# Up projections by seven block products: the first layer too, and when gates, turns and down projections start

## The chip, the cores and the metric

The kernel runs on one core of a Trainium2 chip. The metric is the time of one execution in microseconds (us); shown beside it are the profiled execution and its span, from the first instruction to the last. The engines have short names in the views: PE is TensorE (PEld its weight loads), DVE VectorE, ACT ScalarE, POOL GpSimd, SP the engine that issues the weight loads; PS is the accumulator memory of 8 banks. All numbers are float32. A float32 matmul of the program is two records in the trace ("x16" is eight matmuls).

## The reference, cut to what matters

512 latent tokens of width 1024 pass four layers, and 256 context tokens go with them in layers 0 and 2. In each layer a mixer's output is projected ("out"), weighed by a gate and added; the tokens are normalised, modulated and pass a feed-forward part, whose result is again weighed by a gate and added. What the change touches is the feed-forward part and the gates:

```python
m = silu(c) @ w_mod[i] + b_mod[i]          # shifts, scales and two gates
h = layer_norm(ALPHA * h + g_m * (y @ w_out), ...)
f = square(relu(modulate(h, sh_f, sc_f) @ w1)) @ w2     # layers 0, 1: 1024 -> 4096 -> 1024
h = layer_norm(ALPHA * h + g_f * f, ...)
# layers 2, 3: rms_norm; up 1024 -> 2 * 2816, three-tap convolution along the tokens,
# silu(one half) * other half, down 2816 -> 1024; residual without ALPHA
```

Layer 0 does this for 768 tokens (6 tiles of 128), layer 1 for 512 (4 tiles), layer 2 for 768, layer 3 for 512. Layers 2 and 3 are the second block.

## The kernel before, in words

All weights come through RING, two slots filled in turn by SP; the load for a slot waits until the tile two places earlier is used. Every engine runs a list of its own in a fixed order, and they meet by semaphores: a *flow* is a set of PS buffers with a semaphore "full" (posted by PE) and one "free" (posted by DVE or ACT, first when that engine *offers* the flow).

**Out projection** (`both_halves`, L955 to L982; matmuls recorded at L971): output columns in two halves; in the second half, tile by tile, eight products k of 512 columns. After product k = 7 of tile t PE turns the normalised tile t-1 (`turn_tokens`, eight transposes, L863), which ACT writes to UT with shift and scale (`turned_tokens`, L2481, eight operations). DVE evaluates each tile (`residual`, L1788 and after): product by gate, addition, and for layers 0 and 1 the statistics, the root from ACT (L2488) and two passes of the norm; for layers 2 and 3 ACT squares the tile and takes the root (`rms`, L2557), then DVE scales it (L1860). ACT's order for layers 2 and 3 (`boundary`) is: rms of tile t, then turn of tile t-1. In layers 2 and 3 `conv_columns` (L984) stands behind product k = 3 of the last tile but one (layer 2) or the last (layer 3): PE waits until the tile turned last is in UT, transposes the convolution's vectors (L991), and waits until DVE has copied them (L1775).

**Up projection, layers 1 to 3** (`paired_up`, products at L1016): 256 output columns are a pair. Weights and tokens are cut in 2 by 2 blocks (K in two halves of 4 x 128, columns in two of 128, tokens in two halves), and seven products P1 to P7 stand for eight. PE gives P1 and P2 of pairs 0 and 1 first, with the turn of the last tile between; ACT copies P1 (L2498), and P2 waits for that. DVE makes four sums of tokens for each tile of the second half of the tokens (L2314 to L2317) and four sums of weights for each pair (L2303 to L2306, of pair 0 before the last tile's token sums), and PE's P6 waits for them. DVE then adds up the quarters with seven additions a pair (L2361 to L2377), counted by `quarters_taken`. In layer 1 ACT makes relu and square (L2901, L2902); in layers 2 and 3 DVE makes the convolution (`convolved`, L2338 to L2349).

**Up projection, layer 0** (`up`): eight weight tiles of 512 columns, four chunks each; a chunk is eight matmuls of 512 latent tokens (L926) and eight of 256 context tokens (L928), 32 chunks in all; ACT makes relu and square of 768 tokens (L2887, L2889). The first two chunks go in `early_tile` (L885), latents first.

**Down projection** (`both_halves` again, in four parts of the contraction for each half): PE waits at L1675 for `hidden_ready`, which ACT posts behind the last square (layers 0, 1) and DVE behind the last convolution (layers 2, 3).

**Gates of layer 0**: behind the attention PE transposes them (`gate_rows`, L853), ACT copies them (L2471), POOL stores them to DRAM (L3029) and reads them back on all partitions (L2954, four DMAs); DVE waits for that (L2398) before it offers the flow of the out projection. The attention runs over 40 units in 43 steps, and the rows the gates are made of are complete after step 24.

## Time and profile before

| what | us |
|---|---|
| median of three runs | 4323.12 |
| lowest, highest | 4320.63, 4330.89 |
| the profiled execution, its time | 4322.84 |
| its span | 4321.0 |
| PE busy | 4073.6 (94%) |
| DVE busy | 1690.2 (39%) |
| ACT busy | 813.0 (19%) |

The profile has one core. The page gives busy times and the chain of work that ended last; the chain in order of time gives the long stretches; the timeline shows single instructions, with the idle time of their engine before them in brackets and what ended it; the windows give the granted clock of TensorE in a stretch, 1.00 for 2.4 GHz and 0.50 for 1.2 GHz.

### The profile page before, as it was taken

Reading aid. Unit: us, or ns where it says so; the run is one execution under the profiler, and the core shown is the slowest. Engines: PE = TensorE matmul, PEld = TensorE weight load, DVE = VectorE, ACT = ScalarE, POOL = GpSimd, SP = SyncE. Lnnn points to the kernel's source line nnn. Section 1 sums busy time; section 2 is a strip of 40 time slices with the busy share of each in tenths; the row PEclk is TensorE's granted clock in tenths of the full one; section 3 lists DMA queues with packets and bytes.
Section 4 is the critical chain, followed back from the end, with each engine's and each line's share of the span. In section 5 each row is a group of like instructions: output and inputs, shape, how many; then the busy total and the mean of one; then the engine's idle time right before and its main releaser. Section 6 shows DMA issues by size and latency. Waiting matters only on the chain.

```text
span 4321.0 us, 44906 instructions
## 1 busy us (share of the span) xinstructions
PE 4073.6 (94%) x18144; PEld 2431.1 (56%) x18144; DVE 1690.2 (39%) x2856; ACT 813.0 (19%) x1549; POOL 239.9 (6%) x228
## 2 busy tenths in 40 slices
PE   7998999999999999999999997799998999989999
PEld 6676455544455555458646545545554444758854
DVE  0253400001256555544202028637775015437841
ACT  1265211100122222111102123321100021521000
POOL 1000000000013431300000000000000000000000
PEclk8999999999999999999999997899999999999999
DMA  4255111111112221322223112301111121002222
GB/s 177 102 184 175 49 59 39 58 39 59 33 69 88 81 86 69 118 68 88 88 78 108 38 42 103 133 21 59 59 59 49 54 71 65 1 21 88 87 80 73
DMA packets 192901, 325.68 MB, mean 75 GB/s; under 512 B 4146, under 2 KB 74104, under 8 KB 192576
## 3 DMA queue, kind: packets, MB, share of 16 engines
q1 hardware_dynamic: 186816, 302.00, 20.2%
q0 software_dynamic: 5888, 20.91, 1.5%
q8 instruction: 141, 2.31, 0.2%
q14 instruction: 56, 0.46, 0.0%
HBM read 320.74 MB, written 2.16 MB: 75 GB/s over the span
## 4 chain that ended last, share of the span: by engine, by line
PE 87%; DVE 7%; ACT 3%; issue 1%; DMA 1%; POOL 0%; DVEq 0%; ACTq 0%; SPq 0%
PE PS L971 26%; PE PS L1016 18%; PE PS L926 7%; PE PS L928 3%; PE PS L948 3%; PE PS L885 3%; PE PS L1471 3%; PE PS L1485 2%; PE PS L801 2%; PE PS L1472 1%; PE PS L1632 1%; PE PS L1642 1%; PE PS L1166 1%; PE PS L1135 1%; PE PS L1361 1%
## 5 line engine op out<-in xcount | busy, mean ns | idle before, releaser
L971 PE MATMUL PS<-RING,BIG 128*128 128x512 f32 x2352 | 1022.1, 596 | 22.4 <-DVEq L1721 16.0
L971 PEld LDWEIGHTS PS<-RING,BIG 128*128 128x128 f32 x2352 | 447.6, 191 | 579.8 <-issue 558.7
L1788 DVE TENSOR_TENSOR RES_TMP<-PS,GATE 128x512 f32<-128x512 f32 x80 | 55.3, 692 | 1404.6 <-PE PS L971 1332.5
L1016 PE MATMUL PS<-UT,RING 128*128 128x256 f32 (+1 forms) x1920 | 530.4, 424 | 31.5 <-ACT BIG L2498 15.0
L1016 PEld LDWEIGHTS PS<-UT,RING 128*128 128x128 f32 x1920 | 364.4, 192 | 170.3 <-DVE BIG L2367 22.7
L1016 PE MATMUL PS<-BIG,RING 128*128 128x256 f32 (+1 forms) x1440 | 396.8, 419 | 1.5 <-DVEq L1721 1.1
L926 PE MATMUL PS<-UT,RING 128*128 128x512 f32 x704 | 356.4, 593 | 1.0 <-ACT BIG L2674 1.0
L1016 PEld LDWEIGHTS PS<-BIG,RING 128*128 128x128 f32 x1440 | 273.2, 190 | 96.9 <-DVEq L1721 2.8
L928 PEld LDWEIGHTS PS<-UT,RING 128*128 128x128 f32 x656 | 124.6, 190 | 156.9 <-issue 156.9
L928 PE MATMUL PS<-UT,RING 128*128 128x256 f32 x656 | 195.1, 379 | 0.0
L971 PE MATMUL PS<-RING,UT 128*128 128x512 f32 x320 | 141.5, 601 | 15.7 <-DVEq L1701 14.0
L926 PEld LDWEIGHTS PS<-UT,RING 128*128 128x128 f32 x704 | 133.4, 190 | 30.0 <-issue 12.0
L948 PE MATMUL PS<-RING,UT 128*128 128x512 f32 x320 | 140.1, 600 | 2.5 <-ACT BIG L2766 0.9
L1471 PE MATMUL PS<-UT,RING 128*128 128x512 f32 x256 | 131.1, 594 | 3.3 <-DVE BIG L2126 1.9
L2481 ACT ACTIVATE UT<-PS,COL 128x128 f32<-128x128 f32 x328 | 118.8, 468 | 52.4 <-PE PS L863 49.2
L885 PE MATMUL PS<-UT,RING 128*128 128x256 f32 (+2 forms) x576 | 125.9, 380 | 1.4 <-ACTq L2438 1.4
L801 PE MATMUL PS<-RING,CVW 128*32 128x128 f32 x3072 | 103.5, 291 | 22.5 <-DMA RING<-w_mod_dram 15.7
L1485 PE MATMUL PS<-UT,RING 128*128 128x512 f32 x256 | 120.1, 594 | 0.0
L885 PEld LDWEIGHTS PS<-UT,RING 128*128 128x128 f32 x576 | 99.0, 190 | 26.3 <-issue 16.6
L2191 DVE SCALAR_TENSOR_TENSOR BIG<-PS,BIG 128x510 f32<-128x510 f32 (+3 forms) x176 | 110.5, 628 | 6.2
L971 PEld LDWEIGHTS PS<-RING,UT 128*128 128x128 f32 x320 | 61.0, 193 | 90.0 <-issue 89.4
L1323 PE MATMUL PS<-UT 64*128 64x128 f32 x672 | 73.1, 364 | 38.6 <-DVE GB L2073 24.9
(388 smaller groups left out, 4456.0 us busy)
## 6 DMA issues: line engine op xcount, KB each, us to landing
RING<-w_mod_dram SPq DMA_DIRECT2D x48, 2048.0 KB, 7.9
RING<-ff_w_dram SPq DMA_DIRECT2D x24, 2048.0 KB, 8.0
RING<-w_ffn_up_dram SPq DMA_DIRECT2D x44, 1024.0 KB, 5.0
RING<-ssm_w_in_dram SPq DMA_DIRECT2D x8, 2048.0 KB, 7.7
RING<-ff_w_dram SPq DMA_DIRECT2D x16, 1024.0 KB, 5.3
RING<-w_ffn_down_dram SPq DMA_DIRECT2D x8, 1536.0 KB, 6.6
RING<-w_ffn_down_dram SPq DMA_DIRECT2D x8, 1280.0 KB, 5.8
RING<-ssm_w_out_dram SPq DMA_DIRECT2D x4, 2048.0 KB, 7.8
```

What stands on the lines that cost most here:

```text
L801: ins = mm(bank(bank_, 128)[32 * c:32 * c + 32, :], CVW[:, 4 * k + lc:4 * k + lc + 32], w[:, k, c * 128:(c + 1) * 128], start=k == 0, stop ...
L885: m = mm(PS[:, x + a:x + a + n], w[:, k, c * 128:(c + 1) * 128], UT[:, k, a:a + n], start=k == 0, stop=k == KD - 1)
L926: m = mm(PS[:, x:x + LAT], a, UT[:, k, 0:LAT], start=k == 0, stop=k == KD - 1)
L928: m = mm(PS[:, x + 512:x + 512 + nctx], a, UT[:, k, LAT:LAT + nctx], start=k == 0, stop=k == KD - 1)
L948: m = mm(bank(first_bank + t, cols[1] - cols[0]), inp[:, kk, t * 128:(t + 1) * 128], w[:, k, cols[0]:cols[1]], start=kk == 0, stop=kk == k ...
L971: m = mm(bank(t), inp[:, kk, t * 128:(t + 1) * 128], w[:, k, :], start=kk == 0, stop=kk == kn - 1)
L1016: m = mm(bank(bank_, n), a[:, k, :], b[:, k, :], start=k == 0, stop=k == 3)
L1323: m = mm(bank(b + h % 2, 128, a * 128), kk, qq, start=True, stop=True)
L1471: mm(PS[:, x:x + LAT], a, UT[:, k, 0:LAT], start=k == 0, stop=k == KD - 1)
L1485: m = mm(bank(4 + q), wz[:, k, q * 128:(q + 1) * 128], UT[:, k, 0:LAT], start=k == 0, stop=k == KD - 1)
L2191: ins = V.scalar_tensor_tensor(y[:, lo:hi], PS[:, x + lo + o:x + hi + o], w(k), y[:, lo:hi], ALU.mult, ALU.add)
L2481: step.go(A(UT[:, k, t * 128:(t + 1) * 128], bank(6, 128, k * 128), ACT.Identity, scale=COL[:, w + 1, k, p:p + 1], bias=COL[:, w, k, p:p + ...
```

## The change

What it does:
- Layer 0's up projection becomes `paired_up` with 16 pairs. The seven products are for the 512 latent tokens (256 columns each; `half_tiles` is 2 there and 3 only in layer 2). The 256 context tokens take plain matmuls: 16 per pair (`context`), between P2 and P7, into banks 6 and 7. ACT makes relu of the latent rows (`positive`), relu of the context rows out of PS, and the square of all. Rows of pair 14 are kept in GATE and of pair 15 in GB until the end. Weights come as 16 loads of 1 MB.
- The transposes of layer 0's gates move into step 27 of the attention (`OWN_GATES_STEP`), into a slot of the turned flow.
- In layers 2 and 3 tile t-1 is turned behind product k = 5 of tile t, ACT turns before it squares, and the wait for the copied convolution vectors stands before the next turn.
- DVE makes the sums of weights of pair 0 before the last tile's gating, in all layers.
- The down projection waits at first only for `quarters_taken`, and for `hidden_ready` before the last of the four parts of its first half.
- POOL brings layer 0's second pair of norm vectors behind `hidden_ready`.

```diff
-        PAIRS = {1: 16, 2: NF2, 3: NF2}
+        PAIRS = {0: 16, 1: 16, 2: NF2, 3: NF2}
...
-                if L == 0:
-                    columns(d["ff_w1"][L], 4)
-                else:
-                    pairs(d["ff_w1"][L] if L < 2 else d["w_ffn_up_2"][L - 2], PAIRS[L])
+                pairs(d["ff_w1"][L] if L < 2 else d["w_ffn_up_2"][L - 2], PAIRS[L])
...
+        OWN_GATES_STEP = 27
...
                         if j == len(parts) - 1:
                             steps = [(k, t) for t in range(ntok) for k in range(kc)]
+                            if h == 0 and "rest" in hooks:
+                                hooks["rest"]()
...
-                pe.wait_ge(fb.free, taken[fb] + fb.slots)
...
+            def turn_behind_conv_columns(L, t):
+
+                fb = flow(L, "bias", 1)
                 pe.wait_ge(fb.free, taken[fb] + fb.slots)
+                turn_tokens(L, "f", t)
...
+                def context(p):
+                    f = flow(0, "up", 2)
+                    w = ring((t0 + p) % 2, 8, 256)
+                    b = 6 + place(f)
+                    for c in range(2):
+                        for k in range(KD):
+                            m = mm(bank(b, CTX, c * CTX), w[:, k, c * 128:(c + 1) * 128], UT[:, k, LAT:TOK], start=k == 0, stop=k == KD - 1)
+                    m.then_inc(f.full, 1)
...
                 for p in range(2, PAIRS[L]):
                     one(p)
                     six_and_five(p)
                     two(p)
+                    if L == 0:
+                        context(p)
                     seven_three_four(p)
...
+                    if s_ == OWN_GATES_STEP:
+                        gate_rows(0, 6 + place(tf))
...
-                hooks = {(t, 7): partial(turn_tokens, L, "f", t - 1) for t in range(1, ntok)}
+                hooks = {(t, 7 if L < 2 else 5): partial(turn_tokens, L, "f", t - 1) for t in range(1, ntok)}
...
-                        hooks[ntok - 2 if L == 2 else ntok - 1, 3] = partial(conv_columns, L)
+                        c = ntok - 2 if L == 2 else ntok - 1
+                        hooks[c, 3] = partial(conv_columns, L)
+                        hooks[c, 5] = partial(turn_behind_conv_columns, L, c - 1)
...
-                pe.wait_ge(S("hidden_ready"), nth(L))
...
+                pe.wait_ge(S("quarters_taken"), 7 * (pairs_before(L) + PAIRS[L]))
+                hooks["rest"] = lambda: pe.wait_ge(S("hidden_ready"), nth(L))
...
                 for t in range(ntok):
+                    if which == "m" and t == ntok - 1:
+                        sums_of_weights(L, 0)
                     added(1, t)
...
-                for t in range(ntok // 2 - 1):
+                for t in range(half):
                     sums_of_tokens(t)
-                sums_of_weights(0)
-                sums_of_tokens(ntok // 2 - 1)
...
                     for t in range(ntok):
-                        if L < 2:
-                            root(L, which, t)
-                        else:
+                        if L >= 2:
+                            if t:
+                                turned_(t - 1)
                             rms(L, "f", t, "m_residual_ready", tiles_before(L, "f"))
+                            continue
+                        root(L, which, t)
                         if t:
                             turned_(t - 1)
-                    if L:
+                    if which == "m":
                         first_product(L, 0)
                     turned_(ntok - 1)
...
-                if L < 2:
+                if L == 0:
+                    context(0)
+                    positive(0)
+                    squared(0)
+                    context(1)
+                elif L == 1:
+                    positive(0)
                     squared(0)
...
                     for w, kind in enumerate(("mix", "ff")):
-                        if 2 * n + w:
+                        if L == 0 and w:
+                            pool.wait_ge(S("hidden_ready"), 1)
+                        elif 2 * n + w:
```

## Rows read from the trace of the kernel before

**Rows 1.** The page: the span, and the shares of the chain that ended last.
```profile
span 4321.0 us, 44906 instructions
...
PE 87%; DVE 7%; ACT 3%; issue 1%; DMA 1%; POOL 0%; DVEq 0%; ACTq 0%; SPq 0%
```

**Rows 2.** Chain in order of time (start us, us, what): the long stretches.
```profile
425.26 57.60 PE PS L971 x128
...
848.07 165.04 PE PS L971 x384
...
1915.18 186.99 PE PS L1016 x864
...
2105.02 111.83 PE PS L971 x256
...
3321.16 115.29 PE PS L971 x264
...
4159.22 153.88 PE PS L971 x352
```

**Rows 3.** Timeline from 410 us (start, us, engine, line, what, idle before): the gates.
```profile
410.84 0.38 PE L853 MATMUL PS<-CS,MODC 128*16 128x128 f32 x2 [0.79 <-ACTq L2417]
...
413.94 3.57 POOL L2954 DMA_DIRECT2D GATE<-gates_dram  x4 [1.46 <-DMA gates_dram<-RES_TMP]
...
425.26 5.24 PE L971 MATMUL PS<-RING,UT 128*128 128x512 f32 x6 [14.04 <-DVEq L1701]
```

**Rows 4.** Windows: stretch, us, busy us of five engines, granted clock, DMA share, GB/s.
```profile
406.00:408.00 2.00, 2.00 (x23) 2.00 (x24) 0.23 (x1) 0.60 (x1) 0.00 (x0) 0.57 0.04 8
...
1904.50:1908.00 3.50, 3.42 (x8) 2.63 (x9) 3.36 (x6) 0.00 (x0) 0.80 (x2) 0.53 0.66 225
```

**Rows 5.** Timeline, layer 0: DVE takes the last tile of the out projection.
```profile
513.87 0.69 DVE L1788 TENSOR_TENSOR RES_TMP<-PS,GATE 128x512 f32<-128x512 f32 x1 [1.99 <-PE PS L971]
```

**Rows 6.** Timeline, layer 1: from its last out projection tile to its products.
```profile
1898.05 0.69 DVE L1788 TENSOR_TENSOR RES_TMP<-PS,GATE 128x512 f32<-128x512 f32 x1 [1.99 <-PE PS L1642]
...
1904.58 3.63 PE L1016 MATMUL PS<-UT,RING 128*128 128x256 f32 x8 [3.97 <-ACT BIG L2498]
...
1906.95 0.69 DVE L2303 TENSOR_TENSOR RING<-RING 128x512 f32<-128x512 f32 x1
...
1915.18 1.99 PE L1016 MATMUL PS<-BIG,RING 128*128 128x256 f32 x8 [0.53 <-DVEq L1721]
```

**Rows 7.** Timeline, layer 1: the last addition of its up projection.
```profile
2102.27 0.42 DVE L2377 TENSOR_TENSOR BIG<-BIG,PS 128x256 f32<-128x256 f32 x1 [0.85 <-PE PS L1016]
```

**Rows 8.** Timeline, layer 2: its out projection's end and its first token-sum product.
```profile
2880.97 0.44 PE L991 MATMUL PS<-CS,BIG 44*128 44x44 f32 x4 [1.83 <-ACTq L2438]
...
2881.84 3.70 PE L971 MATMUL PS<-RING,BIG 128*128 128x512 f32 x8 [0.43 <-DVE GB L1775]
...
2893.33 0.69 DVE L1788 TENSOR_TENSOR RES_TMP<-PS,GATE 128x512 f32<-128x512 f32 x1 [3.65 <-PE PS L971]
...
2911.81 2.74 PE L1016 MATMUL PS<-BIG,RING 128*128 128x384 f32 x8
```

**Rows 9.** Timeline, layer 2: the last addition of its up projection.
```profile
3311.74 0.56 DVE L2377 TENSOR_TENSOR GATE<-GATE,PS 128x384 f32<-128x384 f32 x1 [1.44 <-PE PS L1016]
```

**Rows 10.** Timeline, layer 3: the same places, and the work between them.
```profile
3861.78 0.69 DVE L1788 TENSOR_TENSOR RES_TMP<-PS,GATE 128x512 f32<-128x512 f32 x1 [3.87 <-PE PS L971]
...
3864.89 2.90 ACT L2481 ACTIVATE UT<-PS,COL 128x128 f32<-128x128 f32 x8
...
3868.43 3.75 PE L1016 MATMUL PS<-UT,RING 128*128 128x256 f32 x8 [4.16 <-ACT BIG L2498]
...
3873.93 2.90 ACT L2481 ACTIVATE UT<-PS,COL 128x128 f32<-128x128 f32 x8 [5.64 <-PE PS L863]
...
3879.96 1.99 PE L1016 MATMUL PS<-BIG,RING 128*128 128x256 f32 x8 [0.52 <-DVEq L1721]
...
4152.81 0.42 DVE L2377 TENSOR_TENSOR BIG<-BIG,PS 128x256 f32<-128x256 f32 x1 [0.85 <-PE PS L1016]
```

More of the change, by code:

```diff
@@ L184, in build @@
                     nt += 12
-            for name, n in [("out", 4 if L == 1 else 2), ("up", PAIRS.get(L, 8)), ("down", 8)]:
+            for name, n in [("out", 4 if L == 1 else 2), ("up", PAIRS[L]), ("down", 8)]:
                 T0[L, name] = nt
@@ L992, in conv_columns @@
                 m.then_inc(fb.full, 1)
+            def turn_behind_conv_columns(L, t):
+                fb = flow(L, "bias", 1)
                 pe.wait_ge(fb.free, taken[fb] + fb.slots)
[L995 to L1003 removed]
+                turn_tokens(L, "f", t)
             def paired_up(L, old):
                 t0, ntok, n0 = T0[L, "up"], tiles_of(L)[0], pairs_before(L)
[L1008 removed]
+                n = 128 * half_tiles(L)
                 lo, hi = slice(0, 4), slice(4, 8)
@@ L1072, in paired_up @@
                     two(p)
+                    if L == 0:
+                        context(p)
                     seven_three_four(p)
@@ L2470, in gate_rows @@
                 ready(f)
-                give(f, A(gate_rows_of(L), bank(6 if L else 1, 256)[0:16, :], ACT.Copy))
+                give(f, A(gate_rows_of(L), bank(b, 256)[0:16, :], ACT.Copy))
                 post("gate_rows_ready")
@@ L2871, in mixer1, with positive, context @@
                 rooted(SSM_G - 1)
-            def feed_forward(L):
-                f = flow(L, "up", 4)
-                offer(f)
-                hid = hidden(L)
-                t0 = T0[L, "up"]
-                with act.Fori(0, 4, 1) as i:
-                    step.begin(i, 8)
-                    for s in range(2):
-                        for c in range(4):
-                            ready(f, t0 + s if c == 3 else None, i, 6, 2)
-                            x = c * 1024
-                            out = hid[:, bass.ds(i * 8 + s * 4 + c, 1), :].rearrange("p a b -> p (a b)")
-                            act.sem_inc(S("scalar_ticks"), 1)
-                            give(f, A(out, PS[:, x:x + TOK], ACT.Relu), i, 8)
-                            act.sem_inc(S("scalar_ticks"), 1)
-                            step(A(out, out, ACT.Square))
-                step.end(4)
-                got[f] += 24
-                fulls[f] += 18
-                post("hidden_ready")
-            def paired_up(L):
-                def squared(p):
-                    rows = pair_rows(L, p).rearrange("p a n -> p (a n)")
-                    act.wait_ge(S("quarters_taken"), 7 * (p + 1))
-                    step(A(rows, rows, ACT.Relu))
-                    step(A(rows, rows, ACT.Square))
+            def paired_up(L):
+                n0 = pairs_before(L)
+                def positive(p):
+                    rows = pair_rows(L, p)[:, :, 0:LAT]
+                    act.wait_ge(S("quarters_taken"), 7 * (n0 + p + 1))
+                    step(A(rows, rows, ACT.Relu))
+                def squared(p):
+                    step(A(hidden(L)[:, 2 * p:2 * p + 2, :], pair_rows(L, p), ACT.Square))
+                def context(p):
+                    f = flow(0, "up", 2)
+                    ready(f)
+                    give(f, A(pair_rows(0, p)[:, :, LAT:TOK], bank(6 + p % 2).rearrange("p (a n) -> p a n", a=2), ACT.Relu))
                 def gated(j):
@@ L2918, in paired_up @@
                     if L < 2:
-                        squared(p - 1)
+                        positive(p - 1)
+                        if L or p < 15:
+                            squared(p - 1)
+                        if L == 0:
+                            context(p)
                         continue
@@ L2938, in _ @@
                 if L == 0:
-                    gate_rows(L)
-                    offer(flow(L, "up", 4))
+                    offer(flow(L, "up", 2))
                 boundary(L, "m")
-                if L == 0:
-                    feed_forward(L)
-                else:
-                    paired_up(L)
+                paired_up(L)
                 if L in next_of:
```

90 lines of the change are left out of this document (43 added, 47 removed).

## Prediction

> **What bounds the kernel now.** I read the page first: TensorE (PE) is on the chain that ended last for 87% of the span [rows 1]. So a change is worth what it takes from PE's work or from PE's waits, and time on DVE or ACT counts only where PE waits for it. Then the chain in order of time, for the pace of each stretch: the down projection of layer 0 needs 165.04 us for 384 records of 512 columns, 0.430 us a record; the up projection of layer 1, already by seven products, needs 186.99 us for 864 records of 256 columns, 0.216 us each [rows 2]. So 256 columns cost half of 512, and half the columns with the same weights loaded lose next to nothing. Last the timeline around the seams between stretches, for PE's idle time and what ended it, and the windows, for what an idle stretch does to the clock: in layer 1, behind 3.97 us of waiting, eight records took 3.63 us where eight later ones took 1.99 [rows 6], and the granted clock was 0.53 there, that is the level of 1.2 GHz instead of 2.4 [rows 4].
>
> The sums go by the profiled execution (4322.84 us, span 4321.0), which is 0.3 us under the median of the runs, 4323.12. About 0.3% (13 us) is what a measurement of this kernel can tell from no change.
>
> **Layer 0's gates.** Behind the attention PE's first free moment is 410.84, when it transposes the gates; then come ACT's copy, POOL's store and four reads (issued from 413.94), and PE's first out projection matmul is at 425.26, after 14.04 us idle [rows 3]. With the rows stored from step 27 of 43, inside the attention, only the wait for the last unit is left. DVE can offer the flow at once, so the out projection starts at about 410.9: 14.3 us off. The store and the reads go past nothing else on POOL's queue that anybody waits for then (its norm vectors are asked for before them), and SP's weight loads are asked for two tiles ahead. The clock: the six records from 425.26 took 5.24 us instead of 2.6 [rows 3], and the whole stretch 57.60 us where 128 x 0.430 is 55.0, so 2.6 us were lost there [rows 2]. At 406 to 408 the clock is already at 0.57 although PE is busy all the time [rows 4], so the new start may be slow for a while too. Bounds 0 and 2.6 us; I take 1.3, the middle, since no row shows such a start. Added in step 27: the two transposes (0.38 us [rows 3]) and a copy on ACT, which the next turn waits for; bounds 0.4 and 1.5 us, a gain is excluded since nothing leaves the attention; I take 0.5, as PE waits for ACT there anyway. Sum: **15.1 us off**.
>
> **Layer 0's up projection.** Before, from DVE's last out tile at 513.87 [rows 5] to the start of the down projection at 848.07 [rows 2], 334.2 us. It has 32 chunks of 16 records of 512 and 16 of 256 columns; at 0.430 and 0.215 this is 330 us. Now 16 pairs of 56 + 32 records of 256 columns. Step by step:
> - The opening, up to the first P6, has never run in this layer. Layer 1 shows it: from DVE's last out tile at 1898.05 to P6 at 1915.18, 17.1 us, with P1 and P2 of two pairs inside and the waits for ACT between them [rows 6]. Here the token sums need tiles 2 and 3 only, which are turned long before, so the 0.53 us in which PE waited for DVE in front of P6 goes. But the four sums of weights, 4 x 0.69 = 2.75 us [rows 6], now stand before the last gating, where DVE has 1.99 us idle in both layers [rows 5, 6]: the gating, and with it the root, ACT's turn, the copy of P1 and PE's P2, come 0.8 us later. 17.1 - 0.5 + 0.8 = 17.4 us, so P6 at 531.3.
> - The other products: 16 x 56 less the 32 records of the opening are 864, exactly as many as in layer 1's row: 187.0 us [rows 2].
> - The context: 16 x 32 = 512 records at 0.215: 110.0 us. ACT's extra operation and DVE's seven additions lie beside products: a pair now lasts 18.9 us on PE instead of 12.1, and layer 1's pace shows that both engines keep up with the shorter one. Not shown is PE's wait for ACT's new order; bounds 1 us less (864 records at 0.215) and 5 us more for the whole loop (0.3 us a pair), I take 0, layer 1's own pace.
> - The end: the last addition (0.42 us, as in [rows 7]) and the release, 0.6 us.
> The down projection then starts at 531.3 + 187.0 + 110.0 + 0.6 = 828.9: **19.2 us off**. The weights land in half the pieces of before, 1 MB for each pair of 18.9 us, beside PE's work. POOL's late norm vectors have half a down projection (over 160 us) to land in.
>
> Here a page of the Trainium skill speaks against the change. The rows above have 0.216 for 256 columns against 0.430 for 512 [rows 2]. "TensorE: Matmul & The Clock Gate", section "Wait — 56ns, not 53.3ns?", says that each matmul pays about 2.5 ns on top of its columns at 2.4 GHz; by it, an estimate, 864 records would take 186.5 us and the context 110.5. This gives the same sum within 0.1 us, and what it says against narrow matmuls is about 1 us for layer 0.
>
> **The seams of layers 1 to 3.** Up to down: PE now waits for the last addition only. It is followed at once by the first down matmul, which reads rows finished long ago; the squares or the convolution of the last pairs have three parts of the contraction to finish in (over 80 us). The stall's place is taken by nothing that I can find; DVE offers the flow directly behind the last addition.
> - Layer 1: 2102.27 + 0.42 + 0.1 against 2105.02 [rows 2, 7], 2.2 us. The stretch behind took 111.83 us where 256 x 0.430 is 110.0 [rows 2]: 1.8 us of clock that no idle stretch takes any more. In front, the 0.8 us of late gating are lost here too, since P6 waits in the end for the turn of the last tile [rows 6]. Sum: **3.2 us off**.
> - Layer 2: 3311.74 + 0.56 + 0.1 against 3321.16 [rows 2, 9], 8.8 us; clock 115.29 - 264 x 0.430 = 1.8 us. Together 10.6.
> - Layer 3: 4152.81 + 0.42 + 0.1 against 4159.22 [rows 2, 10], 5.9 us; clock 153.88 - 352 x 0.430 = 2.6 us. Together 8.5.
>
> **The openings of layers 2 and 3.** The convolution's transposes waited 1.83 us, and the next product 0.43 us for DVE's copy [rows 8]; both waits go, 2.3 us in each layer. Then layer 3 from DVE's last out tile, 3861.78 [rows 10], in the new order: gating and rms done after 3.1 us (where the row of ACT's turn starts); P1's copy and PE's P2 no longer stand behind that turn, so P2 starts at 3.75 (0.64 us behind ACT's work, as from 3867.79 to 3868.43) instead of 6.65, and behind a short wait it should take 1.75 us and not 3.75; 5.5. The turn of the last tile takes 1.75 us at the low clock (from P2's end to ACT at 3873.93), so 0.9: 6.4. ACT's turn 2.9 and its start 0.1: 9.4. Four token sums and their release, 3.0: P6 at 12.4 instead of 18.2 (3879.96). The turn of the last tile but one (0.9) has moved ahead of that clock's start, so 4.9 us, and **7.2 us** with the convolution. Layer 2: the same, with products of 384 columns; P6 at 13.5 instead of 18.5 (2893.33 to 2911.81 [rows 8]): 4.1 + 2.3 = **6.4 us**. The sums of weights cost nothing here: DVE is idle for 3.65 and 3.87 us before the last gating [rows 8, 10], over the 2.75 that they need. If ACT's new order (turn, then rms) made the rms late, DVE and the next tile's turn would wait; bound 3 us a layer. ACT should be done 0.3 us before the rms is due.
>
> **The sum.** 15.1 + 19.2 + 3.2 + (6.4 + 10.6) + (7.2 + 8.5) = 70.2 us. 4323.1 - 70.2 = **4253 us**.
>
> **The rivals.**
> - *The clock and the handoffs keep part.* The starts at 410.9 and at the down projections stay at the lower level in spite of short waits (2.6 - 1.3, and 6.2 us of the three seams), or the new order in layers 2 and 3 gives only the convolution's share. For it: 0.57 at 406 to 408 with a busy PE [rows 4]. Against it: the out projections run at full pace behind idle stretches of about 2 us. 4253 + 8 to 9 = 4262 us. 15%.
> - *The gates weren't the last wait.* If something else (the first weights, the store's own landing) held the out projection, 14.3 us stay: 4267 us. Against it: the first out matmul is released by DVE's queue, which waits for the reads [rows 3]. 5%.
> - *The change doesn't do what it says in layer 0:* the pair loop gets waits that eat what the eighth product gives, 1.2 us in each of 16 pairs: 4272 us. Against it: in layer 1 the shorter pair runs at 0.216 us a record. 5%.
> - *More than forecast:* layer 0's opening does without the low clock and the context fills small waits of the products: 4246 us. 10%.
> - *Slower:* in each pair of layer 0, PE waits for ACT's copy of P1 behind the new operations. Layer 1's opening shows the price: 3.97 us idle and 1.7 us of low clock [rows 6], 5.7 us a time, 91 us in 16 pairs, more than the 70 us: 4344 us. It decides from 4.4 us a pair. The Trainium skill has this mechanism on the page named above, section "HAM oscillation — how this bites in real kernels": waits that come back between bursts start each burst at half clock. Against it: ACT has some 4 us of work in a pair of 18.9 us. 1%.
>
> **How the numbers follow.** 64% for the forecast, within 4247 to 4259. The range takes in the low bounds of the clock and the first two rivals' times: 4244 to 4268. Faster by over 0.3% (under 4310) are all but the last: 0.98; within 0.3%: 0.01; slower: 0.01.
>
> **What would show it.** Right: the first out matmul of layer 0 at 411 to 412, the down projection of layer 0 starting 33 to 35 us earlier than now, 88 records of 256 columns in 18.9 to 19.1 us, idle times of under 1 us before each down projection and the stretches behind at 0.430 us a record, P6 of layers 2 and 3 some 12.4 and 13.5 us behind the last gating. Wrong: an idle time before each P2 in layer 0's loop, a granted clock under 1.00 in it, an idle PE before turns of layers 2 and 3, a step 27 that grew by over 1.5 us.

## The result and the profile after

The changed kernel takes 4261.9 us against 4325.6 for the kernel before on the same chip (medians of four runs each), a ratio of 0.985, 95% interval 0.984 to 0.987: 63.6 us off where 70.2 were forecast. The profiled execution has a span of 4257.5 us, 63.5 less than before [rows 1]. The page of the changed kernel, its span, busy times and chain:

```profile
span 4257.5 us, 45853 instructions
...
PE 4039.0 (95%) x18528; PEld 2498.0 (59%) x18528; DVE 1786.7 (42%) x3040; ACT 815.5 (19%) x1549; POOL 240.6 (6%) x228
...
PE 88%; DVE 7%; ACT 3%; issue 1%; DMA 1%; POOL 0%; DVEq 0%; ACTq 0%; SPq 0%
```

TensorE bounds it as before. Its chain in order of time shows the same stretches as [rows 2] (L973 was L971, L1013 was L1016, L1064 is the new context product), with the first pairs of layer 0 among them:

```profile
411.02 55.17 PE PS L973 x128
...
541.82 12.09 PE PS L1013 x56
553.90 6.91 PE PS L1064 x32
...
813.73 165.04 PE PS L973 x384
...
2070.46 110.10 PE PS L973 x256
...
3273.72 113.57 PE PS L973 x264
...
4098.23 151.35 PE PS L973 x352
```

Each stretch behind a seam now runs at 0.430 us a record of 512 columns: 55.17 instead of 57.60, 110.10 instead of 111.83, 113.57 instead of 115.29, 151.35 instead of 153.88. The timeline shows how each of them starts, and how little idle time (in brackets) is left. Before, it was 14.04 us in layer 0 [rows 3], and in front of the down projections of layers 1, 2 and 3:

```profile
2105.02 111.83 PE L971 MATMUL PS<-RING,BIG 128*128 128x512 f32 x256 [2.86 <-ACTq L2433]
...
3321.16 115.29 PE L971 MATMUL PS<-RING,BIG 128*128 128x512 f32 x264 [9.53 <-DVEq L1721]
...
4159.22 153.86 PE L971 MATMUL PS<-RING,BIG 128*128 128x512 f32 x352 [6.51 <-DVEq L1721]
```

In the changed kernel:

```profile
411.02 1.53 PE L973 MATMUL PS<-RING,UT 128*128 128x512 f32 x3 [0.78 <-DVEq L1713]
...
813.01 0.42 DVE L2390 TENSOR_TENSOR GB<-GB,PS 128x256 f32<-128x256 f32 x1 [0.85 <-PE PS L1013]
...
813.73 0.67 PE L973 MATMUL PS<-RING,BIG 128*128 128x512 f32 x1 [0.82 <-DVEq L1713]
...
2070.46 1.10 PE L973 MATMUL PS<-RING,BIG 128*128 128x512 f32 x2 [0.73 <-DVEq L1713]
...
3273.72 1.13 PE L973 MATMUL PS<-RING,BIG 128*128 128x512 f32 x2 [0.72 <-DVE GATE L2390]
...
4098.23 1.13 PE L973 MATMUL PS<-RING,BIG 128*128 128x512 f32 x2 [0.58 <-DVE BIG L2390]
```

Where the 63.5 us came from, as differences between the same places of the two profiles (forecast in brackets):

| stretch | us off | forecast |
|---|---|---|
| up to layer 0's output projection, and its clock | 14.2 + 2.4 | 15.1 |
| the rest up to layer 0's down projection | 17.7 | 19.2 |
| layer 0's down projection | 0.0 | 0 |
| layer 1, mixer's opening to product 6 | -1.9 | -0.8 |
| layer 1, product 6 to down; clock behind it | 2.1 + 1.7 | 2.2 + 1.8 |
| layer 1's down to the second piece of layer 2's mixer | -3.4 | 0 |
| layer 2, from there to product 6 | 5.7 | 6.4 |
| layer 2, up to down; clock | 8.8 + 1.7 | 8.8 + 1.8 |
| layer 3, second part of the attention to product 6 | 6.3 | 7.2 |
| layer 3, up to down; clock | 5.6 + 2.5 | 5.9 + 2.6 |
| small pieces between | 0.1 | 0 |

So the parts of the change came within 1.6 us of their forecasts, the gates above and nearly all others a little below, and the largest single loss, 3.4 us, lies where nothing was changed.

### The profile page after: what moved, and what is told of

Its sections match the earlier page's. It is cut to its first block, busy times and chain, and to the rows that moved or that the text cites. A ratio compares the mean times of both kernels' runs of the same rounds, so it can differ in the third digit from the quotient of the medians.

```text
span 4257.5 us, 45853 instructions
## 1 busy us (share of the span) xinstructions
PE 4039.0 (95%) x18528; PEld 2498.0 (59%) x18528; DVE 1786.7 (42%) x3040; ACT 815.5 (19%) x1549; POOL 240.6 (6%) x228
## 4 chain that ended last, share of the span: by engine, by line
PE 88%; DVE 7%; ACT 3%; issue 1%; DMA 1%; POOL 0%; DVEq 0%; ACTq 0%; SPq 0%
PE PS L973 27%; PE PS L1013 22%; PE PS L948 3%; PE PS L1485 3%; PE PS L926 3%; PE PS L1064 3%; PE PS L1499 3%; PE PS L885 2%; PE PS L805 2%; PE PS L1486 1%; PE PS L1646 1%; PE PS L1178 1%; PE PS L1656 1%; PE PS L1337 1%; PE PS L1147 1%
## 5 line engine op out<-in xcount | busy, mean ns | idle before, releaser
L973 PE MATMUL PS<-RING,BIG 128*128 128x512 f32 x2352 | 1016.9, 593 | 3.7 <-DVEq L1713 1.6
L973 PEld LDWEIGHTS PS<-RING,BIG 128*128 128x128 f32 x2352 | 445.5, 190 | 557.1 <-issue 552.2
L1013 PE MATMUL PS<-UT,RING 128*128 128x256 f32 (+1 forms) x2432 | 648.2, 414 | 35.1 <-ACT BIG L2510 18.3
L1013 PEld LDWEIGHTS PS<-UT,RING 128*128 128x128 f32 x2432 | 461.3, 191 | 188.5 <-issue 25.3
L1013 PE MATMUL PS<-BIG,RING 128*128 128x256 f32 (+1 forms) x1824 | 487.6, 410 | 1.5 <-DVEq L1733 1.0
L1013 PEld LDWEIGHTS PS<-BIG,RING 128*128 128x128 f32 x1824 | 346.1, 190 | 107.1 <-DVEq L1733 3.1
L973 PE MATMUL PS<-RING,UT 128*128 128x512 f32 x320 | 139.2, 593 | 2.0 <-issue 1.2
L1485 PE MATMUL PS<-UT,RING 128*128 128x512 f32 x256 | 132.4, 599 | 3.8 <-issue 3.1
L926 PE MATMUL PS<-UT,RING 128*128 128x512 f32 x256 | 127.7, 594 | 1.0 <-ACT BIG L2692 1.0
L805 PE MATMUL PS<-RING,CVW 128*32 128x128 f32 x3072 | 103.4, 292 | 22.6 <-DMA RING<-w_mod_dram 16.7
L2510 ACT ACTIVATE BIG<-PS 128x256 f32<-128x256 f32 (+1 forms) x63 | 25.4, 404 | 505.8 <-PE PS L1013 505.0
L1499 PE MATMUL PS<-UT,RING 128*128 128x512 f32 x256 | 120.1, 594 | 0.0
L2205 DVE SCALAR_TENSOR_TENSOR BIG<-PS,BIG 128x510 f32<-128x510 f32 (+3 forms) x176 | 110.5, 628 | 6.3
L1064 PE MATMUL PS<-UT,RING 128*128 128x256 f32 x512 | 113.1, 379 | 0.0
L948 PEld LDWEIGHTS PS<-RING,UT 128*128 128x128 f32 x320 | 61.6, 193 | 82.7 <-issue 77.0
L805 PEld LDWEIGHTS PS<-RING,CVW 128*32 128x32 f32 x3072 | 89.2, 118 | 32.0 <-issue 22.0
L1064 PEld LDWEIGHTS PS<-UT,RING 128*128 128x128 f32 x512 | 97.3, 190 | 13.2
L973 PEld LDWEIGHTS PS<-RING,UT 128*128 128x128 f32 x320 | 60.0, 190 | 74.2 <-issue 73.2
```

The costliest lines, as they stand in the source:

```text
L805: ins = mm(bank(bank_, 128)[32 * c:32 * c + 32, :], CVW[:, 4 * k + lc:4 * k + lc + 32], w[:, k, c * 128:(c + 1) * 128], start=k == 0, stop ...
L926: m = mm(PS[:, x:x + LAT], a, UT[:, k, 0:LAT], start=k == 0, stop=k == KD - 1)
L948: m = mm(bank(first_bank + t, cols[1] - cols[0]), inp[:, kk, t * 128:(t + 1) * 128], w[:, k, cols[0]:cols[1]], start=kk == 0, stop=kk == k ...
L973: m = mm(bank(t), inp[:, kk, t * 128:(t + 1) * 128], w[:, k, :], start=kk == 0, stop=kk == kn - 1)
L1013: m = mm(bank(bank_, n), a[:, k, :], b[:, k, :], start=k == 0, stop=k == 3)
L1064: m = mm(bank(b, CTX, c * CTX), w[:, k, c * 128:(c + 1) * 128], UT[:, k, LAT:TOK], start=k == 0, stop=k == KD - 1)
```

## The experiments

Each number below is a median with the kernel before on the same chip beside it, or a row of the profile of that kernel.

**The change in parts.** The first three kernels take the kernel before and add one part each; the fourth adds these three, so that only layer 0's up projection is left out.

Gates alone (PE; the copy and POOL's store move with it):

```
+                    if s_ == OWN_GATES_STEP:
+                        gate_rows(0, 6 + place(tf))
...
-                if L == 0:
-                    pe.wait_ge(S("gates_in_columns"), nth(L))
-                    gate_rows(L)
```

> The kernel before with the move of layer 0's gates alone (transposes in step 27 of the attention). My theory, from the two profiles: the out projection starts 14.2 us earlier (411.0 instead of 425.3) and its first stretch takes 55.2 us instead of 57.6, so 16.7 us off, 4307 where before is 4323. Rival one, the full clock behind the attention is luck of that execution: 14.2 us off only. Rival two, the reads of the gates weren't the last wait: under 3 us off.

Measured: 4307.6 against 4327.3, ratio 0.996 (0.994 to 0.997), 19.7 us off where 16.7 were expected. The output projection starts at 408.07 with 0.78 us idle, and its 128 records take 55.17 us:

```profile
408.07 55.17 PE PS L968 x128
...
828.45 165.04 PE PS L968 x384
...
2457.70 9.48 PE PS L1260 x12
```

At the down projection it is 19.6 us ahead of before (848.07 [rows 2]); about 2 us of this were there already at 60 us, ahead of any edit. The rival, that something else held the projection, is out. The last row comes back below: 9.48 us for a piece of layer 2's mixer that took 6.34 in the profile of before:

```profile
2477.26 6.34 PE PS L1261 x12
```

Seams of layers 1 to 3 alone:

```
-                pe.wait_ge(S("hidden_ready"), nth(L))
+                if L == 0:
+                    pe.wait_ge(S("hidden_ready"), nth(L))
+                else:
+                    pe.wait_ge(S("quarters_taken"), 7 * (pairs_before(L) + PAIRS[L]))
+                    hooks["rest"] = lambda: pe.wait_ge(S("hidden_ready"), nth(L))
```

> The kernel before with the new wait of the down projections alone, in layers 1 to 3 (quarters_taken at the start, hidden_ready before the last part of the first half). My theory: the idle times of 2.86, 9.53 and 6.51 us in front of them shrink to 0.6 to 0.8 us, 16.8 us in all, and the low clock behind them goes (1.8, 1.8 and 2.6 us): 22 to 23 us off. Rival, the stretch behind starts at the low clock all the same: 17 us off.

Measured: 4302.9 against 4327.3, ratio 0.994 (0.993 to 0.996), 24.4 us off. By its rows the three seams give 2.1 + 8.9 + 6.0 us and the clock behind them 1.7 + 1.7 + 2.5, in all 22.9, the forecast terms within 0.1 us each.

The orders alone (in layers 2 and 3: turns behind product k = 5, ACT's turn ahead of its rms, the wait for the convolution's vectors ahead of the next turn, the weight sums of pair 0 ahead of the last gating):

```
-                hooks = {(t, 7): partial(turn_tokens, L, "f", t - 1) for t in range(1, ntok)}
+                hooks = {(t, 7 if L < 2 else 5): partial(turn_tokens, L, "f", t - 1) for t in range(1, ntok)}
...
+                    if L >= 2 and which == "m" and t == ntok - 1:
+                        sums_of_weights(L, 0)
```

> The kernel before with the new orders in layers 2 and 3 alone: turns behind product 5, ACT's turn before its rms, the wait for the convolution's vectors moved, and the sums of weights of pair 0 before the last tile there (layer 1 keeps them late). My theory: layer 2's first token-sum product comes 5.6 us and layer 3's 6.5 us earlier, 12 us off. Rival, only the stall at the convolution's transposes goes (2.3 us each): 4.5 us off.

Measured: 4310.2 against 4327.3, ratio 0.996 (0.995 to 0.998), 17.1 us off (the interval is 10 to 20 us), more than the stretches explain: 6.5 us in layer 3, as expected, and 4.1 in layer 2 instead of 5.6, 10.6 in all. Between the two profiles the spans differ by 14.6 us, and 4.1 of these lie ahead of layer 1's product 6, where the two kernels run the same code; the rest of the 17.1 is not explained by the edit.

All three, without layer 0's up projection:

> The three parts together, layer 0's up projection as before. If the parts lie at different places and add up: 16.7 + 22.5 + 12 = 51 us off. The changed kernel is then 17 to 18 us faster than this one by the stretches of layer 0 (402.7 us from the out projection to the down projection where 420.4 would be), less 0.8 us in layer 1. Rival, layer 0's new up projection costs the 4.8 us that the changed kernel's profile shows as low clock at the start of the mixers of layers 1 and 2: then the difference to the changed kernel is 12 us in every run, and this kernel's profile has no low clock there.

Measured: 4275.5 against 4327.3, ratio 0.988 (0.987 to 0.990), 51.8 us off (51 expected). The three parts alone add up to 61.2, so a single part's median is uncertain by some us, and the rows are the better judge. By the medians the changed kernel is 13.6 us faster than this one, between the 17 to 18 of the theory and the 12 of the rival. The rival is half right: in this kernel's profile the clock at the opening of layer 1's mixer is full (7.11 us for the sixteen records, 8.80 in the changed kernel), but the 12 records of layer 2's mixer take 9.47 us here too, without layer 0's new up projection.

Layer 0's up projection alone, on the kernel before:

```
-        PAIRS = {1: 16, 2: NF2, 3: NF2}
+        PAIRS = {0: 16, 1: 16, 2: NF2, 3: NF2}
...
+                    if L == 0:
+                        context(p)
                     seven_three_four(p)
```

> The kernel before with one part of the change alone: layer 0's up projection by seven products of half blocks (with its own end: the down projection waits for the last addition). Gates, openings of layers 2 and 3 and the seams of layers 1 to 3 stay as before. My step says 19.2 us off; the changed kernel and the one with all but this part gave 17.7 between the starts of layer 0's output and down projections. Here the output projection starts late and the clock is low at its start, so expected: from the start of the output projection to the start of the down projection 402 to 405 us (422.8 before), that is 17.5 to 20.5 us off, a time of 4303 to 4309. Rival: the parts help each other (the eighth product's removal only pays where the gates are out of the way), and it gives under 12 us alone.

Measured: 4308.1 against 4325.5, ratio 0.996 (0.994 to 0.997), 17.4 us off. From the start of the output projection to that of the down projection it takes 404.6 us against 422.8, 18.2 off, with the gates where they were, so the part does not need the others:

```profile
424.22 57.56 PE PS L976 x128
...
828.85 165.04 PE PS L976 x384
```

**Is the loop near a wait for ScalarE?** Layer 0's relu done seven times over:

```
                         positive(p - 1)
+                        if L == 0:
+                            for _ in range(6):
+                                positive(p - 1)
```

> The changed kernel, in which ScalarE does each relu of layer 0's up projection seven times over (the result does not change), which adds some 6.4 us of ScalarE work to each of the 16 pairs of blocks. It measures how far the loop is from waiting for ScalarE, which was my rival on the slower side: product 2 of a pair waiting for ScalarE in every pair. My step: ScalarE works 3.5 us of the 18.99 us of a pair, so the added work is hidden: 0 us, at most 1, each pair stays 18.99 us. Rival: the handoff of a pair is in lockstep with TensorE and each relu stands in its path; then a pair grows by 5 to 6.4 us and the whole by 80 to 100 us.

Measured: 4257.2 against 4328.6 for before and 4261.8 for the changed kernel on the same chip: no cost. The windows over one pair (busy us of PE, PEld, DVE, ACT and POOL, then the granted clock), the changed kernel first and then this one:

```profile
541.80:560.80 19.00, 19.00 (x90) 16.73 (x89) 5.62 (x11) 3.41 (x4) 0.00 (x0) 1.00 0.18 56
```

```profile
541.80:560.80 19.00, 19.00 (x90) 16.73 (x89) 5.62 (x11) 9.75 (x10) 0.00 (x0) 1.00 0.18 56
```

ScalarE's work goes from 3.41 to 9.75 us and TensorE stays busy for all 19.00. So the rival on the slower side is not near: 6.3 us more of ScalarE's work in each pair doesn't reach TensorE.

**The weight sums of layers 0 and 1, late again:**

```
-                    if which == "m" and t == ntok - 1:
+                    if L >= 2 and which == "m" and t == ntok - 1:
                         sums_of_weights(L, 0)
...
+                if L < 2:
+                    sums_of_weights(L, 0)
+                sums_of_tokens(half - 1)
```

> The changed kernel with one edit of the change undone, in layers 0 and 1 alone: VectorE builds the weight sums of the first token block behind the token sums of that block again, not ahead of them. My step priced the earlier place at 0.8 us a layer, one tile of four sums ahead of product 6. Expected: product 6 of each of the two layers 0.8 us later against its own last gating row (18.7 us from VectorE's row of the last out tile, against 17.8 to 17.9), and 1.6 us in all; a time cannot show that, the trace can. Rival: product 6 waits for the last token sum alone, and the weight sums before it cost all that VectorE spends on them; then the late place is the better one, and product 6 stands earlier by 1 us or more in each layer.

The expectation has the sign wrong (and misquotes the prediction, which booked the early place as a cost of 0.8 us): the late place is the better one. 4253.4 us in two runs, against 4261.8 for the changed kernel on the same chip. Layer 1 in the timeline, first the changed kernel, then this one:

```profile
1864.98 0.69 DVE L1800 TENSOR_TENSOR RES_TMP<-PS,GATE 128x512 f32<-128x512 f32 x1
...
1871.53 3.75 PE L1013 MATMUL PS<-UT,RING 128*128 128x256 f32 x8 [4.92 <-ACT BIG L2510]
...
1882.74 1.99 PE L1013 MATMUL PS<-BIG,RING 128*128 128x256 f32 x8 [0.52 <-DVEq L1733]
```

```profile
1860.40 0.69 DVE L1800 TENSOR_TENSOR RES_TMP<-PS,GATE 128x512 f32<-128x512 f32 x1 [1.99 <-PE PS L1656]
...
1866.94 3.31 PE L1013 MATMUL PS<-UT,RING 128*128 128x256 f32 x8 [3.97 <-ACT BIG L2513]
...
1877.53 1.99 PE L1013 MATMUL PS<-BIG,RING 128*128 128x256 f32 x8 [0.53 <-DVEq L1733]
```

Late, VectorE is idle 1.99 us before the last gating and takes the tile when it comes; early, it has no idle time there and is 0.9 us late, so that TensorE waits 4.92 us before product 2 instead of 3.97. From the gating to product 6 it is 17.1 us instead of 17.8, so product 6 comes 1.5 us earlier in layer 1, where the rival asked for 1 us or more. With the 0.5 to 1.0 us of layer 0, the two openings explain some 2.5 us of the 8 between the medians; the rest is not explained by this edit, and the early place stands as a small loss.

**The handoff made earlier.** A version that moves the wait itself:

```
-                hooks = {(t, 7 if L < 2 else 5): partial(turn_tokens, L, "f", t - 1) for t in range(1, ntok)}
+                hooks = {(t, 6 if L < 2 else 5): partial(turn_tokens, L, "f", t - 1) for t in range(1, ntok)}
...
+                        if which == "m":
+                            if t:
+                                turned_(t - 1)
+                            if t == ntok - 1:
+                                first_product(L, 0)
+                            root(L, which, t)
+                            continue
...
-                    if which == "m" and t == ntok - 1:
-                        sums_of_weights(L, 0)
+                    if which == "m" and t >= ntok - 2:
+                        half_of_weight_sums(L, 0, t - ntok + 2)
```

> A version meant to beat the changed kernel, at the handoff from the output projection to the up projection, where TensorE still stands idle about 6 us in layers 0 and 1: the turn of the root goes behind product 6 instead of ahead of it, ScalarE turns each tile behind the next one and copies the first product's operand before the root, the weight sums of the first pair are split in two halves that VectorE does before its last two gatings, and in layer 3 the last tile is turned before product 2 of the first pair. If the handoff is a chain of these steps on VectorE and ScalarE, as my step 2 has it: product 6 starts 12.3 us from VectorE's row of the last out tile in layer 0 (17.9 in the changed kernel, 5.6 us less) and 13.0 in layer 1 (17.8, 4.8 less), layer 3 gains 1.2, in all 11 to 12 us, a time of 4249 to 4252. Rival: the root's own latency (the sum over tiles, its turn, ScalarE's root) is what ends the wait and the rearranged steps lay beside it; then the openings move by under 1.5 us each and the whole by under 4 us.

Measured: 4250.4 (4247.6 to 4251.6, five runs) against 4328.6 for before and 4261.8 (4256.5 to 4262.1) for the changed kernel on the same chip; ratio to before 0.982 (0.981 to 0.983). It beats both kernels, by 11.4 us the changed one. Layer 0 in its timeline; the same place in the changed kernel has 4.92 us idle and 3.75 us for these eight records:

```profile
497.24 0.69 DVE L1803 TENSOR_TENSOR RES_TMP<-PS,GATE 128x512 f32<-128x512 f32 x1 [0.61 <-PE PS L973]
...
499.85 1.97 PE L1013 MATMUL PS<-UT,RING 128*128 128x256 f32 x8 [1.00 <-ACT BIG L2526]
...
509.58 1.89 PE L1013 MATMUL PS<-BIG,RING 128*128 128x256 f32 x8
```

The granted clock over the handoff is the reason for somewhat over half of it: the eight records, the turn and the next eight took 3.75, 1.91 and 2.36 us, and take 1.97, 1.09 and 1.89. The changed kernel first (1.2 GHz), then this version (2.4 GHz):

```profile
504.20:510.70 6.50, 6.02 (x18) 5.13 (x19) 5.47 (x8) 0.86 (x3) 0.00 (x0) 0.50 0.01 3
```

```profile
503.00:510.00 7.00, 5.04 (x26) 4.27 (x27) 5.54 (x8) 3.29 (x9) 0.00 (x0) 1.00 0.00 0
```

From the gating to product 6 it takes 12.3 us in layer 0 and 13.0 in layer 1, as expected. In layer 0 this is 5.1 us less and not 5.6, since the changed kernel takes 17.4 us there and not the 17.9 of the expectation. Not all of it arrives: from the start of the output projection to that of the down projection layer 0 gains 4.3 us. The output projection up to product 1 got 0.7 us longer (87.58 instead of 86.85 us, with TensorE busy throughout): a tile with its turn takes 7.86 us where it took 7.74, and the weight loads of each turn now wait for VectorE's norm. Layer 3 gives 0.1 us, not 1.2: its turn and two products fell into a low clock (1.97 us for a turn that takes 1.04).

**The low clock at the openings of mixers.** The changed kernel once more:

> The changed kernel once more, unaltered, on the same chip as the other runs of this call. Two low-clock stretches at the openings of mixers were among what kept its first profile from the forecast: the state product of layer 1's mixer took 8.80 us instead of 7.11, and the two first pieces of layer 2's mixer 53.2 us instead of 49.8. Theory A, chance (the clock falls in short gaps whose place against these instructions is drawn anew in each execution): of these two at least one does not recur, and the profiled span falls at 4252 to 4262. Theory B, a lasting consequence of the change (the code behind layer 0 now meets the fall systematically): both recur, 8.80 and 53.2 within 0.3 us, and the span stays at 4257 or above. The start of layer 0's output projection: the two kernels of the last call with the same gates began it at 407.4 and 408.1, the changed kernel at 411.0; by A it may fall anywhere from 407 to 412.

Measured: 4261.8, span 4260.3. Both stretches recur. Theory A asked that at least one does not, so it missed; theory B missed in the first stretch's size, 10.10 us instead of 8.80 within 0.3, and the second is 53.2 us again. The start of the output projection, 412.24, lies just outside A's 407 to 412. Layer 1's mixer in the changed kernel and in this second execution; then the latter's granted clock; then the same place in the kernel without layer 0's new up projection, which keeps the full clock behind the same idle time:

```profile
1151.63 8.80 PE L1460 MATMUL PS<-UT,RING 128*128 128x512 f32 x16 [3.07 <-issue]
```

```profile
1152.69 10.10 PE L1460 MATMUL PS<-UT,RING 128*128 128x512 f32 x16 [3.42 <-issue]
...
1152.00:1158.50 6.50, 5.81 (x7) 2.52 (x8) 2.38 (x3) 2.33 (x7) 2.75 (x4) 0.50 0.54 94
```

```profile
1166.05 7.11 PE L1452 MATMUL PS<-UT,RING 128*128 128x512 f32 x16 [3.42 <-issue]
```

The sixteen records took 7.11 us, at full clock, in all five kernels with the old up projection of layer 0, behind 3.3 to 3.4 us idle. They took 8.6 to 10.2 us in all eight with the new one, behind 3.1 to 3.6 us idle (the one with layer 0's up alone, 10.02, among them). The next two kernels put throwaway matmuls in front of layer 0's down projection, three and four:

```
+                            if (L, name, h, kk, t) == (0, "down", 0, 0, 0):
+                                for _ in range(3):
+                                    mm(bank(0), inp[:, 0, 0:128], w[:, 0, :], start=True, stop=True)
```

> The changed kernel with three more matmuls of 512 columns in front of layer 0's down projection, whose result the next one overwrites. They shift all that follows by 3 x 0.43 = 1.29 us. Question: why did the clock fall behind the idle 3.1 to 3.5 us at the opening of layer 1's mixer in all five kernels with the new layer 0 (the state product took 8.64 to 10.14 us), and in none of the five with the old one (7.11 each), with the same idle time? Theory A: it hangs on where the gap lies against what the throttle looks at, a matter of a microsecond or two, and the kernels of a kind have it at similar places because the last low stretch before it sets the place. Then the shift moves it away: 7.1 us in this kernel or in the one with four, in both at best. Theory B: it belongs to the new code in some other way (what TensorE does in layer 0): 8.6 to 10.2 us in both.

> The same with four matmuls, a shift of 1.72 us. Theory A: 7.1 us for the state product in this kernel or in the one with three. Theory B: 8.6 to 10.2 us in both.

Measured: 4262.7 and 4267.1. The expectations mis-size the shift: a float32 matmul is two records of 0.43 us, so three and four of them shift the rest by 2.6 and 3.4 us, not by 1.29 and 1.72, and the places in between weren't tried. The fall stays in both:

```profile
1155.22 8.74 PE L1463 MATMUL PS<-UT,RING 128*128 128x512 f32 x16 [3.51 <-issue]
```

```profile
1156.11 10.12 PE L1463 MATMUL PS<-UT,RING 128*128 128x512 f32 x16 [3.41 <-issue]
```

Theory A, as put there, missed in both kernels. This isn't proof of B: where the clock falls in a kernel differs between executions (at 408 to 411 it was 1.00 in the first profile of the changed kernel and 0.50 in the second), so a shift in the program need not be one against the throttle. What ties the fall to layer 0's new products stays open. The fall in layer 2's mixer is another matter: the stretch from the second half of layer 1's down projection to the second piece of layer 2's mixer took 311.6 us in the profile of before and in that of the orders alone, 313.3 with the seams alone and in the two versions with the early handoff (one of them follows below), and 315.0 in the nine others, the gates alone and the kernel without the new layer 0 among them. The cheap case is the rare one, two of fourteen profiles, and the one profile of before that I had happened to show it.

Does the idle time come from a weight tile? In the changed kernel SyncE issues the load of the mixer's second tile at 1147.71, when the last down matmul has left its slot, and TensorE, which waits for two tiles before it uses one, starts at 1151.63. On top of the early handoffs:

```
-                        wb, wc = ring(weights(t0), 8, 128), ring(weights(t0 + 1), 8, 128)
+                        wb = ring(weights(t0), 8, 128)
...
                         turn_tokens(1, "m", 5)
+                        wc = ring(weights(t0 + 1), 8, 128)
```

> The version with the early handoffs, and one edit more, at the opening of layer 1's mixer: there TensorE waits, ahead of its first matmul, for two weight tiles, and the second can be read into its slot only when the last down matmul has left it. In the trace SyncE issues that load at 1147.71, it takes 3.7 us, and TensorE starts at 1151.63. Here TensorE waits for the second tile only behind the eight matmuls that need the first alone and the turn of the last token tile. If this wait makes the gap: the first of the eight starts within 0.6 us of the last turn (3.1 to 3.5 us idle before), the clock stays at 1.00 whatever the place, and the part up to the second eight gets 1.5 us shorter (then the wait for the last tile's norm is what comes last) plus the 1.6 to 3.0 us of low clock: 3 to 4.5 us less than the version without it, 4246 to 4248 us. Rival: the wait is for the turned tokens or a free bank; then the start does not move, and the time is that of the version without the edit, 4249 to 4252.

The mechanism is shown, and the rival, under which the start does not move, is out: no idle time, 7.03 us for the sixteen records, a granted clock of 1.00:

```profile
1145.44 7.03 PE L1463 MATMUL PS<-UT,RING 128*128 128x512 f32 x16
...
1152.31 1.04 PE L863 MATMUL PS<-CS,H 128*128 128x128 f32 x8
...
1145.44:1152.30 6.86, 6.86 (x18) 3.00 (x17) 4.73 (x9) 3.11 (x9) 5.06 (x9) 1.00 0.60 140
```

From the start of the down projection to the next sixteen records it takes 342.4 us instead of 347.7, 5.3 less (3 to 4.5 expected). The gain doesn't last: 4250.9, not the 4246 to 4248 expected, against the 4250.4 of the version without the edit (4325.5 and 4328.6 for before beside them). In the profile 3.5 us are left some 20 us later, 3.3 at 1540, 1.5 at 1600 and none at 1750. The clock is low at 1172 to 1176, at 1574 to 1580 and at 1708 to 1716, where the other version keeps 1.00, and each of the three costs 1.7 to 1.8 us; a low stretch at 1428 to 1432 both versions have. Whether these falls answer to the edit or were drawn can't be told from one profile each.

## Why the prediction was nearly right

*What bounds the kernel.* Right: what was taken from TensorE's waits and work showed up in the stretch behind it, and ScalarE's added work nowhere. It need not show up at the end: the 5.3 us of the late weight tile were gone 600 us later.

*Layer 0's gates: 15.1 forecast, 16.7 in the profile.* The wait was the last one [rows 3]. Of the two unknowns the clock fell better than its middle value: it was full at the new start (2.4 us gained, 1.3 taken). Step 27 fell worse, 0.95 us where 0.5 were taken: from the last transpose ahead of the gates to the attention's next products it takes 2.48 us (337.95 to 340.43), where the kernel before takes 1.53 (337.11 to 338.64), 0.60 us of it waiting. The rest of the surplus is luck with the clock inside the attention, which the sum didn't count: from its last step to PE's first free moment it is 3.8 us instead of 5.4 (406.43 to 410.24, 404.62 to 410.05), and 0.8 us of this had been lost ahead of step 27.

*Layer 0's up projection: 19.2 forecast, 17.7 measured* (18.2 in the experiment with it alone). Two terms, the opening and the loop with its end, were too low by 0.9 and 0.6 us. The opening: the forecast has product 6 at 17.4 us from where the gating could start; it takes 17.4 us from a gating that is 0.9 us late, so 18.3. The half microsecond of waiting for VectorE went, as forecast, and the low clock took it back: the turn and product 1 of the second pair ran 1.91 and 2.36 us, where 1.04 and 1.89 are their times at 2.4 GHz. And the loop: a pair lasts 18.99 us, not 18.9, for the context's records cost 0.216 us like the products', where the forecast took half of 0.430. None of its 512 records waits (the last number is the idle time before them):

```profile
L1064 PE MATMUL PS<-UT,RING 128*128 128x256 f32 x512 | 113.1, 379 | 0.0
```

The Trainium skill, "TensorE: Matmul & The Clock Gate", section "Wait — 56ns, not 53.3ns?", adds about 2.5 ns to each matmul; the estimate by it in the prediction, 110.5 us for the context, agrees with the trace, 16 x 6.91 = 110.6. The estimate counts a float32 record of 256 columns as 512, as 0.430 us for a record of 512 columns suggests (1024 at 2.4 GHz are 0.427).

*The seams.* Right to 0.3 us each, by the table.

*The openings of layers 2 and 3.* The order works as described. In the timeline of layer 2 the convolution's transposes wait for nothing, and product 6 comes 13.8 us behind the last gating (13.5 forecast); in layer 3 it comes after 12.55 (12.4 forecast):

```profile
2846.60 0.44 PE L993 MATMUL PS<-CS,BIG 44*128 44x44 f32 x4
...
2859.41 0.69 DVE L1800 TENSOR_TENSOR RES_TMP<-PS,GATE 128x512 f32<-128x512 f32 x1 [0.84 <-PE PS L973]
...
2873.18 2.74 PE L1013 MATMUL PS<-BIG,RING 128*128 128x384 f32 x8
...
3812.00 0.69 DVE L1800 TENSOR_TENSOR RES_TMP<-PS,GATE 128x512 f32<-128x512 f32 x1 [1.10 <-PE PS L973]
...
3824.55 1.99 PE L1013 MATMUL PS<-BIG,RING 128*128 128x256 f32 x8 [0.52 <-DVEq L1733]
```

*Where the sum was 6.7 us too large.* The time, 4261.9, lies in the range and above the likeliest case's own 4247 to 4259; it equals the rival of 4262, "the clock and the handoffs keep part", but not at the places that it named, where the clock was full, so that this agreement is luck. Of the 6.7 us, 3.4 are the low clock in layer 2's mixer and 1.1 layer 1 up to product 6, where it costs 1.7, both in parts of the program that the change doesn't touch; 1.5 are layer 0's up projection; openings and seams gave 2.3 less in all, 0.1 to 0.9 each; the gates gave 1.6 more. The step that failed is one that the sum left out: it took one profile of before as the price of everything unchanged, and TensorE's clock there is part of what is drawn anew, or pushed, with every edit.

## What to carry to other kernels

Where a helper builds operands ahead of a shared handoff, look at how long its engine is idle before that handoff (1.99 us here): work that exceeds it delays the whole chain (by 0.9 us here), while two halves of it fit before two tiles. Where an engine idles at a handoff, look for a wait taken too early (two tiles awaited where one is used), and count the low clock behind it as a cost that may or may not come. A sum of parts from one profile carries a few us of clock scatter either way: judge a single part by its rows, and take repeated executions of both kernels before explaining less than 0.1%.

## What the runs showed of the hardware

The clock's fall is not a function of the idle time alone: behind 3.31 to 3.42 us idle it stayed at 2.4 GHz in five kernels, and behind 3.07 us in one and 3.42 in another it fell to 1.2 GHz. The Trainium skill, "TensorE: Matmul & The Clock Gate", section "HAM oscillation — how this bites in real kernels", has waits that make each burst behind them start at half clock; of thirteen executions with this wait, eight agree. And in one profile of an unaltered kernel it is low at 408 to 411 with TensorE busy for all of the 3.00 us, in the other it is full there with 2.24 us busy. (In the second everything there comes 1.2 us later, so the windows do not hold the same instructions.) These are the windows, the changed kernel's first profile, then its second:

```profile
408.00:411.00 3.00, 2.24 (x40) 2.01 (x37) 0.85 (x2) 1.02 (x3) 0.00 (x0) 1.00 0.02 5
```

```profile
408.00:411.00 3.00, 3.00 (x32) 3.00 (x30) 0.42 (x1) 0.54 (x2) 0.00 (x0) 0.50 0.02 5
```
